# Two 256-column matmuls in place of one of 512 columns in a float32 weight stream

## What is computed

```
for i in range(DEPTH):                                   # DEPTH = 2
    h = rmsnorm(x, g[0])
    mix = swa_sink_attention(h, ...) if i % 2 == 0 else nsa_attention(h, ...)
    x = x + rmsnorm(mix, g[1])
    h = rmsnorm(x, g[2])
    x = x + rmsnorm(conv_ffn(h, w_gate, w_up, conv_w, conv_b, w_down), g[3])

def conv_ffn(h, w_gate, w_up, conv_w, conv_b, w_down):   # D_FF = 5632
    a = causal_dwconv(h @ w_gate, conv_w, conv_b)
    return (jax.nn.silu(a) * (h @ w_up)) @ w_down

def compress_blocks(kv, pe, w1, b1, w2, b2):             # 15 blocks of 32 positions, 4 groups
    ...
    return jax.nn.gelu(blk @ w1 + b1) @ w2 + b2
```

## Time and profile before

| | |
|---|---|
| time, median of 3 runs | 2331.46 us (2329.56 to 2331.63) |
| profiled execution, its own time | 2332.47 us |
| its span | 2330.8 us |
| PE busy | 2241.0 us, 96% of the span, 12776 matmuls |
| PEld busy | 1919.7 us, 82%, 12776 loads |
| DVE, ACT, POOL busy | 1389.0, 1084.4, 244.1 us |
| mean granted TensorE clock | 0.968 of 2.4 GHz |
| transfers | 375.96 MB, 161 GB/s on average |

### The profile page before, as it was taken

How to read it: one execution, slowest core, us unless ns; L and a number is a source line. 1 busy time by engine, 2 the same in 40 slices (tenths; PEclk the granted TensorE clock), 3 DMA queues, 4 the chain that set the end, 5 groups by cost and what they waited for, 6 DMA issues and landing times.

```text
span 2330.8 us, 36490 instructions
## 1 busy us (share of the span) xinstructions
PE 2241.0 (96%) x12776; PEld 1919.7 (82%) x12776; DVE 1389.0 (60%) x2155; ACT 1084.4 (47%) x1561; POOL 244.1 (10%) x392
## 2 busy tenths in 40 slices
PE   7999999999999999998998999989999999999997
PEld 6777888888888888887897766878888888888886
DVE  5555577676676744448633444566767676664444
ACT  4665554444444444345434555454444444443442
POOL 2251000000000000003002554100000000000000
PEclk9999999999999999999877999999999999999999
DMA  5434535655555555554541221435555555655553
GB/s 187 144 117 136 179 128 175 195 186 183 190 179 195 176 186 183 199 189 128 177 150 38 80 72 64 152 129 181 180 192 175 192 188 179 197 183 187 186 185 109
DMA packets 105716, 375.96 MB, mean 161 GB/s; under 512 B 13475, under 2 KB 13859, under 8 KB 105635
## 3 DMA queue, kind: packets, MB, share of 16 engines
q1 hardware_dynamic: 104290, 373.66, 48.7%
q10 hardware_dynamic: 1344, 1.18, 0.2%
HBM read 372.69 MB, written 2.10 MB: 161 GB/s over the span
## 4 chain that ended last, share of the span: by engine, by line
PE 91%; DVE 4%; issue 2%; ACT 1%; POOL 1%; SPq 0%; DMA 0%; ACTq 0%; DVEq 0%; POOLq 0%
PE set L496 56%; PE set L499 28%; PE set L600 2%; PE set L582 1%; PE set L624 1%; PE set L526 1%; DVE scored L1210 1%; PE set L584 0%; PE set L617 0%; POOL probs L442 0%; PE set L575 0%; DVE block_f L1293 0%; PE set L627 0%; DVE rnorm L1081 0%; DVE xT L1138 0%
## 5 line engine op out<-in xcount | busy, mean ns | idle before, releaser
L496 PE MATMUL set<-hs,whi 128*128 128x512 f32 x3584 | 1286.8, 405 | 46.9 <-DVE hs L1123 20.8
L1049 DVE TENSOR_TENSOR wlo<-raw,whi 128x1024 fp32r<-128x1024 f32 x704 | 854.8, 1227 | 608.2 <-ACT whi L767 608.1
L767 ACT ACTIVATE whi<-raw 128x1024 fp32r<-128x1024 f32 x704 | 737.2, 1056 | 818.0 <-PE set L499 812.5
L499 PE MATMUL set<-hs,wlo 128*128 128x256 f32 x3584 | 980.6, 284 | 0.0
L496 PEld LDWEIGHTS set<-hs,whi 128*128 128x128 f32 x3584 | 669.0, 191 | 204.1 <-DVE hs L1123 22.0
L499 PEld LDWEIGHTS set<-hs,wlo 128*128 128x128 f32 x3584 | 685.8, 191 | 19.9
L496 PE MATMUL set<-hid,whi 128*128 128x512 f32 x1408 | 495.2, 397 | 0.0
L499 PE MATMUL set<-hid,wlo 128*128 128x256 f32 x1408 | 391.0, 281 | 0.0
L496 PEld LDWEIGHTS set<-hid,whi 128*128 128x128 f32 x1408 | 262.3, 188 | 62.5
L499 PEld LDWEIGHTS set<-hid,wlo 128*128 128x128 f32 x1408 | 265.4, 188 | 2.9
L496 PE MATMUL set<-os,whi 128*128 128x512 f32 x512 | 184.8, 406 | 0.0
(11 more groups left out here) (163 smaller groups left out, 1390.7 us busy)
## 6 DMA issues: line engine op xcount, KB each, us to landing
raw<-in_stream SPq DMA_DIRECT2D x704, 512.0 KB, 3.5
xT<-in_x SPq DMA_DIRECT2D x4, 512.0 KB, 5.5
out_y<-xT SPq DMA_DIRECT2D x8, 256.0 KB, 2.0
wg_raw<-in_w_gates ACTq DMA_DIRECT2D x1, 768.0 KB, 5.3
w2k_sb<-in_w ACTq DMA_DIRECT2D x2, 128.0 KB, 5.8
conv_sb<-in_conv SPq DMA_DIRECT2D x1, 176.0 KB
w2v_sb<-in_w ACTq DMA_DIRECT2D x1, 128.0 KB, 5.1
g_sb<-in_gains SPq DMA_DIRECT2D x1, 64.0 KB
```

The costliest lines, as they stand in the source:

```text
L496: return mm(bank[:, 0:2 * w], whi[:, slot, cols], r, start=first, stop=final)
L499: return mm(bank[:, w:2 * w], wlo[:, slot, cols], r[:, 0:w], start=False, stop=False)
L767: A(whi[:, slot, :], raw[:, slot, :], ACT.Copy).then_inc(hi_ready, 1)
L1049: V.tensor_tensor(wlo[:, slot, :], raw[:, slot, :], whi[:, slot, :].bitcast(F32), ALU.subtract).then_inc(lo_ready, 1)
```

## The change

Inside a sum, each `high` matmul other than the sum's first and last is issued as two: one over the first `w` columns into the first half of the bank, one over the second `w` columns into the second half, both with the same stationary tile of `whi`. `low` stays as it is. The sum's first matmul (which begins the accumulation) and its last (which ends it) keep `2 * w` columns. The function is the same for all sources, so the compression units with `w` = 60 are split too.

```
 def high():
-    return mm(bank[:, 0:2 * w], whi[:, slot, cols], r, start=first, stop=final)
+    if first or final:
+        return mm(bank[:, 0:2 * w], whi[:, slot, cols], r, start=first, stop=final)
+    mm(bank[:, 0:w], whi[:, slot, cols], r[:, 0:w], start=False, stop=False)
+    return mm(bank[:, w:2 * w], whi[:, slot, cols], r[:, w:2 * w], start=False, stop=False)
```

## The result

The changed kernel takes 2361.28 us (median of four runs, 2360.76 to 2362.92) against 2330.93 us (median of four). The ratio is 1.0132, its 95% interval 1.0115 to 1.0150: 30 us slower. The prediction was 2370 us, with a range of 2345 to 2393.

The account below looks back on a forecast made before the run. The prediction took TensorE's weight-stream matmuls as the bound. On the profiled execution 2332.5 + 14.8 (stream) + 24 (compression units) = 2371.3 us, or 2370 us against the median; range 2345 to 2393.

Parts of the forecast that it names:

- The bound: Weight stream on TensorE: what a matmul costs more or less goes nearly one for one into the span.
- (a): Every split: a second matmul on the same stationary tile adds a 128x128 weight load, 0.112 us at the high clock.
- (b): Weight stream: each of 4928 splits costs 3 ns, what a matmul costs beyond its columns; +14.8 us.
- the low matmul is just that already: Weight stream: the 256-column low matmul, 0.119 us with one load under it, stands for each part; 0.357 us a pair.
- (c): Compression units, 1144 to 1195 us: bound by loads, a third load lengthens a pair to 0.64 us; +24 us.
- (d): Attention units: 224 splits cost 0.7 us in each layer, some of which may go into waits for POOL and DVE.
- The faster one: Rival, weight stream: equal short matmuls follow at the load's pace, 0.336 us for three, -84 us; 2271 us; 7%.
- The second load: Rival, all splits: the second load isn't made or is hidden altogether, so the compression units lose nothing; 2346 us; 6%.
- No instruction packet: Rival, feed-forward loops: 368 matmuls no longer fit where instructions are kept, jumps wait for fetches; +36 to +63 us; 8%.
- The contending load: Rival, weight stream: with three loads in a pair, reading weights overlaps longer with reading columns and slows them; 2405 us; 4%.

Follow-up runs that it names:

- the padded kernels: Kernel before with 240 and 180 columns streamed in the compression units instead of 120 and 60: 2310.68 us; the same with the high matmul there split: 2318.76 us.

## Why the prediction was right, and where it was off

**The bound.** That a matmul's cost in the stream goes nearly one for one into the span holds: with 384 + 128 columns a pair had 0.405 - 0.353 = 0.052 us more, 4928 of them are 256 us, and the kernel took 261 us longer.

**(a) A load for each part.** Right: 17816 loads, 5040 more. The row that told it was the four loads of the same ones.

**(b) The stream.** Right in mechanism, too large in size: 1.7 ns a split instead of 3. By that the term is 8.4 us, not 14.8; the trace has 3.6 + 2.2 = 5.8 us of it and of the clock drops. The subtraction 119 - 116 was sound for the kernel before: its starts give 118.7 - 115.8 = 2.9 ns. What was off is the step "the low matmul is just that already". A 256-column matmul between 512-column ones takes 118.7 ns, among equals 118.3; three times this difference is what lies between 2.9 and 1.7 ns. Why it is 0.4 ns shorter, no run shows. The range of +10 to +20 us for this term was too narrow. Against the profile of before the terms were 38.8 us and 28.8 were measured. Of the 10 us between them 6.4 come from this term, 1.0 from the compression units, and up to 2.7 from clock drops outside them that happened to be shorter, for which there was no term.

**(c) The compression units.** +23.0 us against +24 forecast. The 46 matmuls of the first 5 us at the high clock are 15 pairs, as assumed, and the rest goes at 0.64 us. That the clock wouldn't rise was right, and the padded kernels show that the halved clock made the term so large: at 1.00 the same splits cost 7.4 us, or 11.5 with the waits that they hid.

**(d) The attention.** The waits for POOL and DVE are much as they were (9.2 and 7.3 us, 8.4 and 7.3 before). What the prediction did not price is that the attention of layer 1 takes 273 to 279 us in one and the same kernel, with fewer or more clock drops. A cost of 6 us there is as large as the term of the stream.

**The rivals.** The faster one would have needed three short matmuls to run at the pace of the loads; they run at that of their columns, 0.118 us. The second load exists. No instruction packet was moved in the loop of layer 0 although its body has grown from 256 to 368 matmuls; from 420 to 800 us the only queue in the changed kernel's trace is this one:

```profile
q1 hardware_dynamic: 19308, 70.30, 55.8%
```

The same holds for the loop of layer 1, from 1690 to 2085 us:

```profile
q1 hardware_dynamic: 20128, 73.30, 55.9%
```

The contending load would have shown in slower columns; with 118.3 ns instead of 118.7 they are not slower.

## What to carry to other kernels

Cutting a matmul in two repeats its weight load even if the weights are the same, and whether this costs is decided for each matmul by itself: the load lies under the one matmul that runs ahead of it, so each part needs enough columns to cover a load (here 256 were just enough, 224 were not). Before a change is made in a shared function, look for the callers with small shapes: 2% of the splits made four fifths of the loss, because there the loads were the bound already, and at half clock. And where a stretch is bound by weight loads at a halved clock, streaming more columns than needed can make it faster; here it was worth 20 us, more than the change cost in its stream.

## What the runs showed of the hardware

- A weight load of 128 columns takes 0.112 us at a granted clock of 1.00 and 0.213 us at 0.50. The clock fell to 0.50 and stayed there for 69 us in the changed kernel while TensorE's loads were busy 64.00 of 64.00 us and its matmuls had 60 columns; with 120 and 180 columns, and the loads busy 40.90 of 40.90 us, it stayed at 1.00. The Trainium skill, page "TensorE: Matmul & The Clock Gate", section "LDWEIGHTS (loading the stationary operand)", gives P / 1.2 ns with P the columns of the stationary tile, 128 here, an estimate of 107 ns. The trace is near it at the high clock, and at the low clock it is twice that.
- Only one load is prepared: it starts with the matmul before its own, and a longer matmul doesn't let a second one start (384 + 128 columns: 0.405 us a pair instead of 0.355). The Trainium skill, page "TensorE: Matmul & The Clock Gate", section "Step-by-step: what each phase is for", says that the load of the next tile runs while this tile's matmul runs. The runs agree, and add that it is the next one only.
- A recorded start of a matmul doesn't wait for its load. With 384 + 128 columns the low matmul is listed at 1100.89, 0.06 us after the 128-column part, though its load began at 1100.83; its successor comes 0.17 us later instead of 0.12. The waiting lies inside the listed matmul, so distances of single matmuls mislead where loads bind; those of whole pairs don't. The low matmul's own 0.34 us, instead of 0.28 before, fit that.
- In this fp32r stream 256 more columns in a matmul cost 115.8 ns, 8 to 9% more than at one column in each cycle of 2.4 GHz (106.7 ns). It was the same with one row tile streamed throughout and with ACT and DVE writing a sixteenth. What does it was not found.
